# Residual additions and squares moved ahead of the weight splits, and the sum of squares and the root's table prepared earlier

## The reference, cut to what matters

```
rms(x)      = x * rsqrt(mean(x*x) + EPS)
modulate(x) = rms(x) * (1 + scale) + shift
h  = modulate(x, sh1, sc1)                      # norm 1
z  = h @ w_in                                   # four token mixers are built from z
x  = x + g1 * (sum_i sigmoid(h @ w_gate[i] + b_gate[i]) * (o_i @ w_branch[i])) @ w_out
h2 = modulate(x, sh2, sc2)                      # norm 2
x  = x + g2 * ((silu(g) * a) @ w_down)          # a, g = dwconv3(h2 @ w_up), width 2816 each
```

## Time and profile before

| | us |
|---|---|
| three runs | 2503.54, 2502.26, 2506.65 (median 2503.54) |
| profiled execution | 2500.07, of which the trace spans 2498.4 |
| TensorE busy | 2307.5 (92%), 12802 matmuls |
| VectorE busy | 1339.0 (54%) |
| ScalarE busy | 955.4 (38%) |
| GpSimd busy | 159.6 (6%) |

### The profile page before, as it was taken

How to read it: one execution, slowest core, us unless ns; L and a number is a source line. 1 busy time by engine, 2 the same in 40 slices (tenths; PEclk the granted TensorE clock), 3 DMA queues, 4 the chain that set the end, 5 groups by cost and what they waited for, 6 DMA issues and landing times.

```text
span 2498.4 us, 34870 instructions
## 1 busy us (share of the span) xinstructions
PE 2307.5 (92%) x12802; PEld 1911.7 (77%) x12802; DVE 1339.0 (54%) x1880; ACT 955.4 (38%) x1383; POOL 159.6 (6%) x170
## 2 busy tenths in 40 slices
PE   5989998899999889999999978799999997999998
PEld 5767866788888768888888866586778876878776
DVE  6455456566667365425524455536745555545444
ACT  3454456422223253213312344445633334423232
POOL 2112001000000000000000001210100000000000
PEclk9899999999999989999999989899999998999999
DMA  6111110244444211111121131120145552222222
GB/s 270 43 42 51 60 38 18 76 136 143 135 143 145 82 40 61 59 59 59 59 67 55 64 111 59 51 68 21 43 143 173 170 171 67 93 93 85 92 93 101
DMA packets 58509, 221.20 MB, mean 89 GB/s; under 512 B 6608, under 2 KB 6608, under 8 KB 57760
## 3 DMA queue, kind: packets, MB, share of 16 engines
q1 hardware_dynamic: 44384, 160.46, 19.3%
q0 software_dynamic: 14016, 59.26, 6.9%
HBM read 214.45 MB, written 5.24 MB: 88 GB/s over the span
## 4 chain that ended last, share of the span: by engine, by line
PE 84%; ACT 5%; DVE 5%; issue 3%; DMA 2%; DVEq 1%; SPq 0%; ACTq 0%
PE PS L575 81%; PE PS L825 3%; ACT XY L970 1%; ACT TM L970 1%; ACT W_hi L970 1%; DMA RA<-w_ada 1%; DVE XY L1281 1%; DVE F_lo L1278 1%; ACT F_hi L970 1%; DVE RA L1281 0%; DVE TM L1281 0%; ACT RA L970 0%; DMA XY<-x_in 0%; DVEq L435 0%; DVE W_lo L1278 0%
## 5 line engine op out<-in xcount | busy, mean ns | idle before, releaser
L1278 DVE TENSOR_TENSOR W_lo<-W_st,W_hi 128x1024 fp32r<-128x1024 f32 x278 | 344.7, 1241 | 821.5 <-ACT W_hi L970 801.5
L575 PE MATMUL PS<-H_hi,W_hi 128*128 128x512 f32 x2240 | 687.7, 364 | 68.1 <-DVE H_lo L1278 36.7
L575 PE MATMUL PS<-H_lo,W_hi 128*128 128x512 f32 x2240 | 674.4, 358 | 0.0
L575 PE MATMUL PS<-H_hi,W_lo 128*128 128x512 f32 x2240 | 673.8, 358 | 0.0
L970 ACT ACTIVATE W_hi<-W_st 128x1024 fp32r<-128x1024 f32 x278 | 293.7, 1057 | 903.1 <-PE PS L575 893.6
L575 PEld LDWEIGHTS PS<-H_hi,W_hi 128*128 128x128 f32 x2240 | 376.0, 193 | 144.5 <-issue 71.4
L575 PEld LDWEIGHTS PS<-H_lo,W_hi 128*128 128x128 f32 x2240 | 374.2, 193 | 64.9 <-issue 1.7
L575 PEld LDWEIGHTS PS<-H_hi,W_lo 128*128 128x128 f32 x2240 | 372.3, 192 | 63.1
L575 PE MATMUL PS<-F_hi,W_hi 128*128 128x512 f32 (+1 forms) x952 | 290.7, 360 | 26.5 <-DVE F_lo L1278 14.5
L575 PE MATMUL PS<-F_lo,W_hi 128*128 128x512 f32 (+1 forms) x952 | 287.6, 356 | 0.0
L575 PE MATMUL PS<-F_hi,W_lo 128*128 128x512 f32 (+1 forms) x952 | 287.2, 356 | 0.0
(11 more groups left out here) (130 smaller groups left out, 2081.1 us busy)
## 6 DMA issues: line engine op xcount, KB each, us to landing
W_st<-w_all SPq DMA_DIRECT2D x278, 512.0 KB, 3.4
RA<-w_mod POOLq DMA_DIRECT2D x40, 512.0 KB, 3.6
TM<-w_mod POOLq DMA_DIRECT2D x40, 512.0 KB, 3.8
RA<-w_ada SPq DMA_DIRECT2D x8, 512.0 KB, 8.8
XY<-bias_na POOLq DMA_DIRECT2D x2, 1792.0 KB, 8.1
RA<-w_mod SPq DMA_DIRECT2D x6, 512.0 KB, 8.3
XY<-x_in SPq DMA_DIRECT2D x4, 768.0 KB, 11.5
x_spill<-XY POOLq DMA_DIRECT2D x1, 3072.0 KB, 10.3
```

The lines of the kernel that those rows point to most:

```text
L575: return nc.tensor.matmul(o, lhsT, rhs, start=start, stop=stop)
L1278: return nc.vector.tensor_tensor(o, a, b, f)
```

## The change

In out_tiles VectorE does the addition to x (and in the phases with squares the addition of the square) first and `used`, with its split_lo, after. In the phases with squares ScalarE waits for the addition and squares the tile first, and does `used`, with its split_hi, after; in the others ScalarE is as before. VectorE's loop has its last round written out in the phases with squares. TT holds seven squares; the eighth is summed by TensorE, which reads SQ[1] in a second product into the same PSUM. TensorE's norm has no `begin` any more. ScalarE runs one Abs_reciprocal_sqrt on a single column ahead of the norm's `begin`. GpSimd's sum at the start has six additions instead of seven.

```diff
 # GpSimd, start
-            for k in range(1, KT):
+            for k in range(1, KT - 1):
 # TensorE
             def squares_of_x(w):
-                pe.wait_ge(S["sq_sum"], base["sq_sum"] + KT - 1)
+                pe.wait_ge(S["sq_sum"], base["sq_sum"] + KT - 2)
                 for s0, sn in segs(w):
-                    ins = mm(pair(3)[:, s0:s0 + sn], MT[:, M_ONE, :], TT[:, s0:s0 + sn], True, True)
+                    mm(pair(3)[:, s0:s0 + sn], MT[:, M_ONE, :], TT[:, s0:s0 + sn], True, False)
+                pe.wait_ge(S["sq"], base["sq"] + KT)
+                for s0, sn in segs(w):
+                    ins = mm(pair(3)[:, s0:s0 + sn], MT[:, M_ONE, :], SQ[1][:, s0:s0 + sn], False, True)
                 ins.then_inc(S["ss"], 1)
-            def norm(ph, w, summed=False):
+            def norm(w, summed=False):
                 if not summed:
-                    begin(pe, ph, "act", "dve")
                     squares_of_x(w)
 # ScalarE
             def norm(ph, w, sc, sh):
+                op(SM[:, 57:58], EPSB, ACT.Abs_reciprocal_sqrt)
                 begin(act, ph, "pe", "dve")
...
                     for u in range(2):
-                        used(i, 2, b0 + u, stop=final)
                         if squares:
                             act.wait_ge(S[name], i * 2 + (base[name] + u + 1))
                             wait(act, "sq_sum", 0 if first(i) else i * 2 + (base["sq_sum"] + u - 1))
                             op(SQ[u][:, 0:w], XY[:, bass.ds(i * (2 * T) + u * T, w)], ACT.Square).then_inc(S["sq"], 1)
+                        used(i, 2, b0 + u, stop=final)
 # VectorE
                     for u in range(2):
-                        used(i, 2, b0 + u, stop=final)
+                        dve.wait_ge(S["block_done"], i * 2 + (b0 + u + 1))
                         if reloads and not first(i):
                             dve.wait_ge(S["x_reloaded"], 16 * reloads)
...
                         ins.then_inc(S[name], 1)
-                        if squares:
-                            if first(i) and u == 0:
-                                continue
-                            dve.wait_ge(S["sq"], i * 2 + (base["sq"] + u + 1))
+                        if squares and u == 0 and not first(i):
+                            dve.wait_ge(S["sq"], i * 2 + (base["sq"] + 1))
+                            dve.wait_ge(S["sq_sum"], i * 2 + (base["sq_sum"] - 1))
+                            tt(TT[:, 0:w], TT[:, 0:w], SQ[0][:, 0:w], ALU.add).then_inc(S["sq_sum"], 1)
+                        if squares and u == 1 and not (last(i)):
+                            dve.wait_ge(S["sq"], i * 2 + (base["sq"] + 2))
                             if first(i):
                                 tt(TT[:, 0:w], SQ[0][:, 0:w], SQ[1][:, 0:w], ALU.add).then_inc(S["sq_sum"], 1)
                             else:
...
+                        used(i, 2, b0 + u, stop=final and last_phase)
```

More of the change, by code:

```diff
@@ L68 @@
 ada_used scale_acc mod_step silu_c cc_loaded par_loaded rope_loaded const_loaded sg_loaded bias_loaded mask_loaded mask_step
-adab_loaded cb_silu mod_acc mod_fold sq_sum x_head x_reloaded x_spilled out_stored
+adab_loaded eps_set cb_silu mod_acc mod_fold sq_sum x_head x_reloaded x_spilled out_stored
 sq ss y0 newton norm_u norm_v norm_hi norm_lo
@@ L630, in squares_of_x @@
             def squares_of_x(w):
-                pe.wait_ge(S["sq_sum"], base["sq_sum"] + KT - 1)
+                pe.wait_ge(S["sq_sum"], base["sq_sum"] + KT - 2)
                 for s0, sn in segs(w):
-                    ins = mm(pair(3)[:, s0:s0 + sn], MT[:, M_ONE, :], TT[:, s0:s0 + sn], True, True)
+                    mm(pair(3)[:, s0:s0 + sn], MT[:, M_ONE, :], TT[:, s0:s0 + sn], True, False)
+                pe.wait_ge(S["sq"], base["sq"] + KT)
+                for s0, sn in segs(w):
+                    ins = mm(pair(3)[:, s0:s0 + sn], MT[:, M_ONE, :], SQ[1][:, s0:s0 + sn], False, True)
                 ins.then_inc(S["ss"], 1)
-            def norm(ph, w, summed=False):
+            def norm(w, summed=False):
                 if not summed:
-                    begin(pe, ph, "act", "dve")
                     squares_of_x(w)
-                base.advance(sq_sum=KT - 1)
+                base.advance(sq_sum=KT - 2)
                 base.advance(**norm_counts())
@@ L947, in _ @@
                 end(pe, "pe")
-                norm(p0 + PH_NORM1, T, summed=l == 0)
+                norm(T, summed=l == 0)
                 end(pe, "pe")
@@ L958, in _ @@
                 end(pe, "pe")
-                norm(p0 + PH_NORM2, w)
+                norm(w)
                 end(pe, "pe")
@@ L1253, in _ @@
             squares_of_x(T)
+            act.wait_ge(S["eps_set"], 1)
             for l in range(DEPTH):
@@ L1604, in body, with last @@
                             else:
-                                dve.wait_ge(S["sq_sum"], i * 2 + (base["sq_sum"] + u - 1))
-                                tt(TT[:, 0:w], TT[:, 0:w], SQ[u][:, 0:w], ALU.add).then_inc(S["sq_sum"], 1)
-                repeat(dve, KT // 2, body, peel_last=last_phase)
+                                dve.wait_ge(S["sq_sum"], i * 2 + base["sq_sum"])
+                                tt(TT[:, 0:w], TT[:, 0:w], SQ[1][:, 0:w], ALU.add).then_inc(S["sq_sum"], 1)
+                        used(i, 2, b0 + u, stop=final and last_phase)
+                def last(i):
+                    return isinstance(i, int) and i == KT // 2 - 1
+                repeat(dve, KT // 2, body, peel_last=last_phase or squares)
                 done[0] += KT
@@ L1657, in ffn @@
                     end(dve, "dve")
-            nc.vector.memset(EPSB, EPS)
+            nc.vector.memset(EPSB, EPS).then_inc(S["eps_set"], 1)
             for l in range(DEPTH):
```

## The result

The changed kernel took 2488.84 us (median of five, 2483.64 to 2496.24), the kernel before 2503.54 (five, 2499.71 to 2507.09): ratio 0.994, 95% interval 0.9917 to 0.9964. Faster, then, and by twice what was forecast: 15 us in place of 7. Both were run again later: the changed kernel twelve times (median 2486.19), the kernel before 35 times beside it (2499.27), ratio 0.9955 [0.9936, 0.9974], so 11 us, between 6.5 and 16. One more execution of the kernel before took 2941.5 us at a mean granted clock of 0.745 and is left out of every median and ratio here. The profiled execution after took 2483.64 (span 2482.0); the one before 2500.07, so this pair differs by 16.4.

The account below looks back on a forecast made before the run. The prediction took TensorE, in 84% of the chain of waits, as the bound. Its terms summed to -6.85, so -7: 2493.1 us for the profiled execution, 2496.5 by the median of runs, range 2489.5 to 2502.

Parts of the forecast that it names:

- norm 2 of layer 0: Root of this norm was to start near 873.0 instead of 877.92: gain 4.9 us, bounds 3.5 to 6.0.
- norm 2 of layer 1: Same reckoning with 512 columns: root 4.3 us behind the last block instead of 8.2, gain 3.9, bounds 2.8 to 5.
- norm 1 of layer 1, held by sg_bs: Root about 5.2 us earlier, but TensorE waits for sg_bs landing behind x's spill: gain only 1.0, bounds 0 and 5.2.
- norm 1 of layer 0: At the kernel's start, TensorE's second sum costs 2.2 us, table load saves 1.28: net loss 0.9, bounds -0.2 to +1.6.
- group starts, the gaps: TensorE's waits at four feed-forward group starts shorten by 1.05 or 0.65 us each: gain 3.4, bounds 2.8 to 4.3.
- x comes back, the gaps: Where x returns by DMA, splits queue behind addition and square: loss 2.1 plus 1.85 us, sum 3.95, bounds 3.3 to 4.5.
- the clock: TensorE's slow stretch behind the longer gap where x returns in layer 0: loss 1.5 us; nothing given for group starts.
- The clock at those gaps: Step pricing TensorE's clock behind changed gaps: 0.7 chance of losing 2.1 us at layer 0's x return, taken as +1.5.
- (A): Norm 1 of layer 1: sg_bs landing doesn't hold TensorE, so 5.2 us gained there; sum -11, 2492.5 us; chance 0.12.
- (B): Shorter gaps keep TensorE's clock at most of four group starts; sum -13, 2490.5 us; chance 0.13.
- (C): Table load ahead fails or drains first, so roots come 1.3 to 1.4 us later in three norms; 2500.5 us; chance 0.12.
- (D): Later splits make TensorE wait within phases with squares, 0.6 us a tile; +12, so 2508 us; chance 0.05.

Follow-up runs that it names:

- groups_only: Kernel before with only VectorE's addition moved ahead of its split in the out_tiles phases without squares; 2491.39 us, ratio 0.9965 to the kernel before.
- groups_undone: Changed kernel with the old order, split then addition, in the out_tiles phases without squares; 2495.56 us, ratio 0.9985 to the kernel before.
- before_again: Kernel before, unchanged, run again for a second profile and more times; 2496.75 us, ratio 1.0004 to the runs beside it.
- after_again: Changed kernel, unchanged, run again for a second profile and more times; 2486.19 us, ratio 0.9955 to the kernel before.
- sg_first: Changed kernel with the three spatial-gating loads put on the POOL queue ahead of the spill of x; 2481.28 us, ratio 0.9917 to the kernel before.
- no_table_ahead: Changed kernel without the single-column Abs_reciprocal_sqrt ahead of the norms; 2490.73 us, ratio 0.9959 to the kernel before.
- keep_busy: Changed kernel with extra, unread matmuls in TensorE's idle times at the norms and group starts; 2479.06 us, ratio 0.9908 to the kernel before.

## Why the prediction was wrong

The direction was right, the size too small; 2488.84 lies below the range.

| step | forecast | in the profiles |
|---|---|---|
| norm 2 of layer 0 | -4.9 | -5.1 |
| norm 2 of layer 1 | -3.9 | -4.2 |
| norm 1 of layer 1, held by sg_bs | -1.0 | -0.4 |
| norm 1 of layer 0 | +0.9 | +0.5 |
| group starts, the gaps | -3.4 | -3.4 |
| x comes back, the gaps | +3.95 | +4.3 |
| sum of the chain | -8.35 | -8.3 |
| the clock | +1.5 | -5.4 (the table of starts, summed) |
| TensorE's pace at full clock | not named | -2.2 |
| the profiled pair | -6.85 | -16.4, of which -8.3 - 5.4 - 2.2 = -15.9 |

That the three come so near to the whole is partly luck, for other places cancel in this pair: the stretches from the first down tile to the next group, at paces of their own (-1.1 and +1.1), the starts behind the two norms 2 (+0.6 and -0.7 of clock), and layer 1 between its first input tile and the return of x (+0.15).

**The step that failed** is "The clock at those gaps": "The gaps of the four group starts fall to 2.5, where by these rows either can happen, and I give nothing for it." If either can happen where before the clock was nearly always lost, about half of it is gained, and half of four times 1.8 is 3.6; groups_only and groups_undone, with the loss at each start, give 3.2. I had priced the same chance where it counted against the change (x comes back, +1.5) and not where it counted for it. The same step puts layer 1's return of x at nothing because its start "was slow already"; the longer gap cost 0.9 more of clock there (1.7 lost before, 2.6 to 2.7 after). And two starts behind gaps that the change leaves alone (2.16 and 3.04 us, layer 1) are not in it at all.

Taken over the two profiles of each kernel (before and before_again, after and after_again) the clock's terms are: group starts -4.3, x comes back +2.05 and +0.9, and in layer 1 two starts behind unchanged gaps of 2.16 and 3.04 us, slow in both profiles of the kernel before and in neither of the changed one, -1.55 and -1.6. That is -4.5. With the means over all kernels of this study (-3.2 for the groups, and some -0.4 for the gap of 3.04, which was slow in eight of the nine other kernels with the changed norm) it is -2.2. With the chain's -8.3 this makes -10.5 to -12.8, and the larger sample measured -11.2; from the median of the runs shown before that is 2492.3, inside the range. What lay beyond is the first sample's luck, of which the last section shows a source. The larger sample's interval, 6.5 to 16, holds the forecast 7 too: that the clock terms were missing is shown by the losses read in the traces, not by the times.

**The start** of norm 1 of layer 0 rose to full clock sooner than I took: eight f32 matmuls took 4.72 (42.27 to 46.99), not 2.9 + 2.2.

**The rivals.** (A), sg_bs not binding, is refuted: it bound more than before, and sg_first shows what it held back. (B), the shorter gaps keep the clock, came half true, at 3.2 in place of 6, and its time, 2490.5, was the nearest. (C) is refuted by the order of the rows in norm 2 and by no_table_ahead. (D) is refuted: of TensorE's five waits for W_lo two are where x comes back, and the three others (3.20, 1.68 and 3.21 us) lie in the stages behind norms and stand in the kernel before too (3.22, 1.69 and 3.20).

**Still open.** Why the start of the up phase in layer 1, behind 2.16 us of idle time, was slow (1.6 to 1.7 lost) in before, before_again, groups_only and keep_busy and in none of the ten other profiles, at the same gap. The first three share the old norm 2; keep_busy has the changed one, with extra matmuls in it. So what TensorE did some 20 us earlier may bear on it; nothing was tried on it.

## What to carry to other kernels

Price a shorter idle time of TensorE twice, once for the gap and once for the clock behind it, with the same chance for a gain as for a loss. Where a norm or another dependent chain is shortened, look which small transfer stands behind a large one on the same queue: it becomes the next bound. An order that is right inside a loop can be wrong in its first round, where another thing (a transfer) is late; treat that round by itself.

## What the hardware showed that was not expected

**TensorE has two paces at full clock.** Both windows lie in one long stage of matmuls, with granted clock 1.00; first the kernel before, then the same kernel again (before_again):

```profile
470.00:800.00 330.00, 329.61 (x1901) 288.02 (x1900) 216.90 (x295) 98.64 (x111) 24.32 (x46) 1.00 0.41 136
```
```profile
470.00:800.00 330.00, 330.00 (x1870) 286.05 (x1869) 211.22 (x288) 96.23 (x109) 24.43 (x46) 1.00 0.41 134
```

1901 and 1870 matmuls in 330 us. Read from the starts of the rows, a pair of 512 and 256 columns begins every 346.7 ns in the one and every 353.3 ns in the other: the rows last 0.51, 0.51, 0.51 in the quick pace and 0.51, 0.51, 0.53 in the slow one, so that every third pair is some 20 ns late (by the starts: 361, 349, 350 ns, again and again, against 343 and 350 in turn). The pace mostly changes where a stage does and holds within one, and it differs between executions of one kernel. In the profiled pair it favoured the kernel after in the first up phase (before, then after):

```profile
910.00:1030.00 120.00, 119.64 (x678) 103.62 (x678) 65.70 (x88) 39.01 (x42) 0.00 (x0) 1.00 0.19 64
```
```profile
910.00:1030.00 120.00, 119.64 (x691) 105.29 (x690) 66.51 (x88) 40.33 (x44) 0.00 (x0) 1.00 0.20 66
```

This is 2.2 us in that stage, and 6.5 over the merge stage between before and before_again. Two of the fourteen profiles have the slow pace in this long stage, before_again and groups_only, and both executions took long for their kernel (2508.90 against a median of 2496.75, and 2498.85 against 2491.39). So the pace is one source of the spread of executions (before_again's had 2489.17 to 2511); that it is the main one is not shown. Five runs are too few for a change of 7. What sets the pace is open; nothing was tried on it.

**The clock behind a gap does not go by its length alone.** Behind 2.5 to 2.6 us it was lost in 18 of 32 starts; but at the second group's start of layer 1 in eight of eight profiles, and at the third's in one of eight, with the same 2.50 us and the same releaser. Behind 3.24 to 3.35 us, at a down phase of layer 0, it was kept in three of 14. So something beside the gap's length decides; what it is was not tried.
